# Latent attention's projections as three products of split halves, with the query input written first

## The reference

```python
h = modulate(rmsnorm(x, g_in), shift, scale)          # key side, own shift and scale
kv = h @ w_a                                          # 1024 -> 256 + 64
c_kv, k_rope = jnp.split(kv, [B_KV_LORA], axis=-1)
c_kv = rmsnorm(c_kv, g_latent)
kvb = (c_kv @ w_b).reshape(B_, S, B_HEADS, B_NOPE + B_V)
k_nope, v = jnp.split(kvb, [B_NOPE], axis=-1)
k_rope = apply_rope(k_rope, cos, sin)
...
cq = rmsnorm(h @ w_q_a, g_q_latent)                   # query side, 1024 -> 384
q = (cq @ w_q_b).reshape(B_, S, B_HEADS, B_NOPE + B_ROPE)
q_nope, q_rope = jnp.split(q, [B_NOPE], axis=-1)
```

## Time and profile before

| | before |
|---|---|
| time of three runs | 1122.48, 1123.25, 1126.98 us; median 1123.25 |
| span of the profiled execution | 1122.2 us (no other time is listed for that execution; the median lies 1.05 us above it) |
| TensorE busy | 1051.8 us, 94% |
| VectorE busy | 717.4 us, 64% |
| ScalarE busy | 499.2 us, 44% |
| mean granted TensorE clock | 0.986 |
| HBM read | 202.58 MB, 181 GB/s over the span |

### The profile page before, as it was taken

How to read it: one execution, slowest core, us unless ns; L and a number is a source line. 1 busy time by engine, 2 the same in 40 slices (tenths; PEclk the granted TensorE clock), 3 DMA queues, 4 the chain that set the end, 5 groups by cost and what they waited for, 6 DMA issues and landing times.

```text
span 1122.2 us, 19655 instructions
## 1 busy us (share of the span) xinstructions
PE 1051.8 (94%) x8476; PEld 881.5 (79%) x8476; DVE 717.4 (64%) x1180; ACT 499.2 (44%) x792; POOL 33.2 (3%) x31
## 2 busy tenths in 40 slices
PE   5999999889998989999988999999899889999997
PEld 5884679887787867787766999999557769999995
DVE  6778248738889757655596776776335756644444
ACT  2424132136643576444364535454323745544542
POOL 0000015200000100000000000000000000000000
...
DMA packets 15078, 204.88 MB, mean 183 GB/s; under 512 B 1800, under 2 KB 1800, under 8 KB 2832
## 3 DMA queue, kind: packets, MB, share of 16 engines
...
HBM read 202.58 MB, written 1.05 MB: 181 GB/s over the span
## 4 chain that ended last, share of the span: by engine, by line
PE 78%; DVE 12%; ACT 4%; DMA 3%; issue 2%; SPq 0%; DVEq 0%; ACTq 0%
PE bank L434 15%; PE bank L436 14%; PE bank L435 14%; PE bank L529 8%; PE bank L393 5%; PE bank L745 5%; DMA ring<-in_stream 3%; DVE slot_parts L1846 3%; DVE small L1820 2%; PE bank L542 2%; PE bank L556 2%; PE bank L650 1%; PE bank L729 1%; ACT page_parts L1245 1%; DVE arena L2284 1%
## 5 line engine op out<-in xcount | busy, mean ns | idle before, releaser
L434 PE MATMUL bank<-page_parts 128*128 128x512 f32 (+1 forms) x1104 | 377.4, 342 | 8.6 <-DVE slot_parts L1846 3.8
L1846 DVE TENSOR_TENSOR slot_parts<-ring,page_parts 128x2048 fp32r<-128x2048 f32 x104 | 237.2, 2289 | 115.3 <-ACT page_parts L1245 114.7
L1245 ACT ACTIVATE page_parts<-ring 128x2048 fp32r<-128x2048 f32 x104 | 197.8, 1913 | 133.9 <-PE bank L436 73.2
L434 PEld LDWEIGHTS bank<-page_parts 128*128 128x128 f32 x1104 | 209.9, 190 | 32.8 <-issue 7.5
L436 PE MATMUL bank<-page_parts 128*128 128x512 f32 x576 | 225.1, 391 | 0.0
L435 PE MATMUL bank<-slot_parts,page_parts 128*128 128x512 f32 x576 | 225.0, 391 | 0.0
L1302 ACT ACTIVATE arena<-bank 128x512 f32<-128x512 f32 (+2 forms) x134 | 73.8, 574 | 193.6 <-PE bank L529 70.4
L435 PE MATMUL bank<-page_parts 128*128 128x256 f32 x528 | 149.4, 283 | 0.0
L436 PE MATMUL bank<-page_parts,slot_parts 128*128 128x256 f32 x528 | 149.4, 283 | 0.0
L436 PEld LDWEIGHTS bank<-page_parts 128*128 128x128 f32 x576 | 108.5, 188 | 22.9
L435 PEld LDWEIGHTS bank<-slot_parts,page_parts 128*128 128x128 f32 x576 | 108.6, 189 | 21.5
...
## 6 DMA issues: line engine op xcount, KB each, us to landing
...
pos_i<-in_positions ACTq DMA_DIRECT2D x1, 1.0 KB, 4.0
```

Of the source, the lines that this page charges most:

```text
L434: mm(out, a[0], b[0], start=start, stop=False)
L1245: act(unit_parts(n)[0], unit_values(n)[1], ACT.Copy).then_inc(ac.step("w_hi"), 1)
L1846: tt(unit_parts(n)[1], lo, hi, ALU.subtract).then_inc(dv.step("w_lo"), 1)
```

## The change

Every projection of the latent attention (cq, ckv, qr, qn, kn, v3) now takes split operands and `three`. Its panels are cut into units of unequal size (`split_spans`: 1536, 1536; 1280, 1280, 1536; 1536, 1536; 2048, 2048 columns) and split by ScalarE and VectorE as the MLP's are; q_a's two units are split at the end of the first MLP. The two modulated inputs are split on VectorE (`split_mixed`), the turned latents get a high part from ScalarE (`latent_hi`) and a low part from VectorE (`latent_lo`, straight from PSUM). ScalarE writes the whole query input before the key input. TensorE computes half of qn before the key latent is turned, the other half after.

The diff, cut to its core:

```diff
+            def split_spans(name, *spans):
+
+                order.append([name, None])
+                i = panels[0]
+                panels[0] += 1
+                for n, (a, b, k, on) in enumerate(spans):
+                    units.append({"slot": i, "span": (a, b, k), "page": on, "stage": stage[0], "panel": order[-1], "last": n == len(spans) - 1})
+                return len(units) - len(spans)
 
             stage_first = {}
...
             transposes("hT_d", XN)
             ada_turned()
-            project_tok(("cq",), wt(panel("q_a"), QL), hT2, n=QL, transposed="hT_d")
-            panel_used()
+            stage[0] = "mla"
+            q_a = split_spans("q_a", (0, 1536, 4, 15), (1536, 3072, 4, 16))
+            unit_of["cq"] = q_a
+
+            def latent(name, units_of, src, n, wait):
+
+                bs = [claim((name, tb)) for tb in range(TB)]
+                for i in range(units_of):
+                    W = use_unit()
+                    for tb in range(TB):
+                        unit_of[name, tb] = unit_at[0] - 1
+                        for k in range(4 * i, 4 * i + 4):
+                            if tb == 0 and k % 2 == 0:
+                                pe.wait_ge(sem(wait), k // 2 + 1)
+                            ins = three(bs[tb][:, 0:n], [a[:, k, tb * P:(tb + 1) * P] for a in src], [w[:, k - 4 * i, :] for w in W],
+                                        k == 0, k == KT - 1)
+                        if i == 1 and tb == 0:
+                            ins.then_inc(filled((name, 0)), 1)
+                    ins.then_inc(unit_used((name, 1) if i else None), 1)
+
+            def columns_of(name, half, W, rows, src, last):
+
+                for i in range(2):
+                    b = claim((name, half, i))
+                    unit_of[name, half, i] = unit_at[0] - 1
+                    for hf in range(2):
+                        ct = 2 * i + hf
+                        for k, row in enumerate(rows):
+                            ins = three(b[:, hf * T:(hf + 1) * T], [w[:, row, ct * P:(ct + 1) * P] for w in W], [a[:, k, :] for a in src],
+                                        k == 0, k == len(rows) - 1)
+                    ins.then_inc(unit_used((name, half, i)) if last and i else filled((name, half, i)), 1)
+
+            def rows_of(product, W, rows, src, last):
+
+                for tb in range(TB):
+                    p = (*product, tb)
+                    b = claim(p)
+                    unit_of[p] = unit_at[0] - 1
+                    for k, row in enumerate(rows):
+                        ins = three(b[:, :], [a[:, k, tb * P:(tb + 1) * P] for a in src], [w[:, row, :] for w in W], k == 0, k == len(rows) - 1)
+                    ins.then_inc(unit_used(p) if last and tb else filled(p), 1)
+
+            latent("cq", 2, split_parts(HQ_PAGES), QL, "hT_q_split")
             spread(2)
-            Wa = panel("kv_a")
-            project_tok(("ckv",), wt(Wa, KVL + RD), hkvT2, n=KVL + RD)
+            unit_of["kv_a"] = split_spans("kv_a", (0, 1280, 4, 2), (1280, 2560, 4, 14), (2560, 4096, 3, 15))
+            latent("ckv", 2, split_parts(HKV2_PAGES), KVL + RD, "hT_kv_split")
             pe.wait_ge(sem("cq_n"), 1)
             transposes("cqT", CQ, tiles=3)
-
-            project_tok(("qr",), Wa[:, 2560:4096].rearrange("p (k n) -> p k n", k=3), CQT, k_tiles=3, transposed="cqT")
-            panel_used()
+            W = use_unit()
+            for i in range(2):
+                pe.wait_ge(*evacuated(("cqT", i)))
+            rows_of(("qr",), W, range(3), CQT_PARTS, True)
+            unit_of["q_b"] = split_spans("q_b", (0, 1536, 3, 16), (1536, 3072, 3, 14))
+            columns_of("qn", 0, use_unit(), range(3), CQT_PARTS, True)
             pe.wait_ge(sem("ckv_n"), 1)
             b = claim("ckvT")
             for j in range(2):
...
+            columns_of("qn", 1, use_unit(), range(3), CQT_PARTS, True)
+            unit_of["kv_b"] = split_spans("kv_b", (0, 2048, 4, 15), (2048, 4096, 4, 16))
+            pe.wait_ge(*evacuated("ckvT"))
+            W = use_unit()
             for half in range(2):
-                project_T(("qn", half), Wn[:, half * 1536:(half + 1) * 1536].rearrange("p (k n) -> p k n", k=3), CQT, k_tiles=3)
-            panel_used()
-            Wb = panel("kv_b")
-            pe.wait_ge(*evacuated("ckvT"))
+                columns_of("kn", half, W, (2 * half, 2 * half + 1), CKVT_PARTS, half == 1)
+            W = use_unit()
             for half in range(2):
-                project_T(("kn", half), Wb[:, half * 1024:(half + 1) * 1024].rearrange("p (k n) -> p k n", k=2), CKVT, k_tiles=2)
-            for half in range(2):
-                project_tok(("v3", half), Wb[:, 2048 + half * 1024:2048 + (half + 1) * 1024].rearrange("p (k n) -> p k n", k=2),
-                            CKVT, k_tiles=2)
-            panel_used()
+                rows_of(("v3", half), W, (2 * half, 2 * half + 1), CKVT_PARTS, half == 1)
             ada(3, rest=2)
             pe.wait_ge(sem("qr_rope"), 1)
             transposes("qrT", QR, tiles=4)
...
+                    split(unit_of["cq"] + 1)
...
 
 
             act_.wait_ge(sem("mod"), 4)
-            for i in range(4):
-                act_.wait_ge(*finished(("hT_d", i)))
-                for jj in range(2):
-                    j = 2 * i + jj
-                    for n, (dst, m) in enumerate(((hkvT2, 2), (hT2, 3))):
+            for dst, m in ((hT2, 3), (hkvT2, 2)):
+                for i in range(4):
+                    act_.wait_ge(*finished(("hT_d", i)))
+                    for jj in range(2):
+                        j = 2 * i + jj
                         ins = act(dst[:, j, :], bank(("hT_d", i))[:, jj * T:(jj + 1) * T], ACT.Identity,
                                   scale=MODS[m][0][:, j:j + 1], bias=MODS[m][1][:, j:j + 1])
-                        if (jj, n) == (1, 1):
-                            ins.then_inc(ac.frees(("hT_d", i)), 1)
-                        else:
+                        if jj == 0:
                             ins.then_inc(ac.step(), 1)
-            ada_turned()
+                    ins.then_inc(ac.frees(("hT_d", i)) if m == 2 else ac.step("hT_q"), 1)
+                if m == 3:
+                    split(unit_of["kv_a"])
+                    ada_turned()
+            split(unit_of["kv_a"] + 1)
             for tb in range(TB):
                 copy(CQ[:, tb, :], ("cq", tb), QL)
             for tb in range(TB):
                 copy(CKVR[:, tb, :], ("ckv", tb), KVL + RD)
-            scaled("cqT", CQT, par("q_latent"), tiles=3)
+
+            def latent_hi(product, parts, scale, tiles, first=0):
+
+                act_.wait_ge(*finished(product))
+                for j in range(tiles):
+                    act(parts[0][:, first + j, :], bank(product)[:, j * T:(j + 1) * T], ACT.Copy, scale=scale[:, first + j:first + j + 1]).then_inc(
+                        ac.step("latent_hi"), 1)
+
+            latent_hi(("cqT", 0), CQT_PARTS, par("q_latent"), 2)
+            latent_hi(("cqT", 1), CQT_PARTS, par("q_latent"), 1, 2)
             for tb in range(TB):
                 copy(QR[:, tb, :], ("qr", tb))
-            act_.wait_ge(*finished("ckvT"))
-            for j in range(2):
-                ins = act(CKVT[:, j, :], bank("ckvT")[:, j * T:(j + 1) * T], ACT.Copy, scale=par("kv_latent")[:, j:j + 1])
-                if j == 0:
-                    ins.then_inc(ac.step(), 1)
-            ins.then_inc(ac.frees("ckvT"), 1)
+            for i in range(2):
+                copy(QNT[:, 2 * i:2 * i + 2, :], ("qn", 0, i))
+            latent_hi("ckvT", CKVT_PARTS, par("kv_latent"), 2)
             pair(KRT_OF, "krT", T)
-            for half in range(2):
-                for i in range(2):
-                    copy(QNT[:, 4 * half + 2 * i:4 * half + 2 * i + 2, :], ("qn", half, i))
+            for i in range(2):
+                copy(QNT[:, 4 + 2 * i:6 + 2 * i, :], ("qn", 1, i))
             for half in range(2):
                 for i in range(2):
                     copy(KNT[:, 4 * half + 2 * i:4 * half + 2 * i + 2, :], ("kn", half, i))
...
+            def split_mixed(name, pages, ready):
+
+                value, (hi, lo) = page(pages[0], KT), split_parts(pages)
+                for i in range(4):
+                    js = slice(2 * i, 2 * i + 2)
+                    dve.wait_ge(*ready(i))
+                    V.tensor_copy(hi[:, js, :], value[:, js, :]).then_inc(dv.step(), 1)
+                    dve.wait_ge(*dv.last)
+                    tt(lo[:, js, :], value[:, js, :], hi[:, js, :].bitcast(F32), ALU.subtract).then_inc(dv.step(name + "_split"), 1)
+
+            def latent_lo(product, parts, scale, tiles, done, first=0):
+
+                dve.wait_ge(sem("latent_hi"), done + tiles)
+                for j in range(tiles):
+                    hi, lo = (a[:, first + j, :] for a in parts)
```

(13 more changed lines are left out.)

21 lines of the change are left out of this document (14 added, 7 removed).

## The result

The changed kernel takes 1129.24 us (median of 18 runs, 1125.28 to 1134.58) against 1125.99 us of the kernel before on the same chips (18 runs, 1121.97 to 1127.89). The ratio is 1.0031, 95% interval [1.0018, 1.0043]: within the 0.5% that the prediction counts as no change, though the interval lies above 1. Forecast was 2.55 us on top of the median of the runs shown (0.23%), that is 1125.8. The profiled execution spans 1128.0 us against 1122.2.

What follows compares the result with a forecast made beforehand. TensorE was taken to bound the stage. The walk's +0.2 us and clock drops' +2.4 gave +2.6 on the 1122.2 span, 1124.8, or 1125.8 on the runs' median; own range 1121.5 to 1128.9, 8-in-10 range 1120.0 to 1129.5.

Steps and rivals of the forecast that it cites:

- TensorE's bill: The six latent-attention projections: three reduced-precision matmuls per product take 39.7 us instead of 48.5, relieving TensorE of 8.8 us.
- steps 1 and 2: Stage's beginning: cq ends at 820.8 us instead of 824.3, ckv at 829.7 instead of 834.7.
- step 2: VectorE up to the query statistics: TensorE wins five microseconds, but VectorE's cq is only 1.0 us ahead of before.
- VectorE's bill: Splitting inputs, panels and latents adds 22.9 us on VectorE in the stage, against 31.7 us of room.
- Step 3: Before qr: TensorE stands 3.9 us for VectorE's splits and low parts; qr starts at 835.1 us, before at 836.34.
- Step 4: At the key latent's turn: VectorE stands 3.4 us; its panel sums end at 867.2 us instead of 859.14.
- the walk: Each engine followed in written order through the stage: attention starts at 870.1 us against 869.91, +0.2, good to 2 us.
- Step 5: After v3, ending at 859.7 us: TensorE stands 1.5 and 5.1 us for the sums' columns; scores start at 870.1.
- The clock: After the 3.9 and 5.1 us stalls TensorE's clock drops, costing 0 to 1.7 us each, taken as 1.2: +2.4.
- Rival B: TensorE's clock stays low after the stalls, 6.8 us a drop, costing 3.4 each: +7.0, 1130.3 us; chance 0.14.
- Rival A: If the panel sums were not last, TensorE's 6.6 us in the stage would stay won: 1116.7 us; chance 0.10.
- Rival C: The stalls in the stage take the gain exactly and no clock drop falls on work: 1123.5 us; chance 0.20.

Runs made afterwards that it cites:

- e10_late_only: The changed kernel with cq and ckv put back to full precision, their inputs and panels not split; ratio to the kernel before 1.004.
- e1_warm: The changed kernel with matmuls that nobody reads put into TensorE's three stalls; ratio to the kernel before 0.9998.
- e3_turn_first: The changed kernel with the key latent turned ahead of the first half of qn again; ratio to the kernel before 1.0038.
- e4_sums_gap: The changed kernel with 6 of 16 panel-sum steps moved into VectorE's wait ahead of the key latent's low part; ratio to the kernel before 0.9966.
- e2_no_sums: The changed kernel with 12 of the 16 steps of the two panel sums ahead of the attention left out; ratio to the kernel before 0.997.

## Why the prediction was right

- **Size and sign.** 0.23% slower was forecast, 0.31% [0.18, 0.43] measured. In microseconds it was closer: 1129.24 lies within the 8-in-10 range by 0.3, and above the 1128.9 that was the forecast's own upper bound and its border to "slower". The kernel before measured 1125.99 here, 2.7 above the median of the three runs shown, which is most of the distance to 1125.8; that this shift did not carry the time out of the range is luck, the difference of 0.31% against 0.23% is not.
- **TensorE's bill and steps 1 and 2.** cq was done at 821.1 (823.06 less 1.95), forecast 820.8; ckv's end some 830.1, forecast 829.7. The column prices between the rows' 0.2276 and 0.1215 us held: cq's 48 products start over 8.26 us, 47 times 0.176. Of the 5 us won on cq and ckv VectorE's query statistics show 1.0 (828.09 less 1.95 is 826.1, against 827.16), as step 2 said, and e10_late_only shows qr's start to hang on that split by 0.8.
- **VectorE's bill.** The low parts, for which no row stood, took 0.42 us each (1.26 for three), 0.44 (0.88 for two): within the bounds of 0.3 and 0.69, and above my 0.36.
- **Step 3.** Stall 3.84, forecast 3.9; qr at 835.26 on the scale of before, forecast 835.1.
- **Step 4.** The wait for the key latent was 5.39 instead of 3.4 us, and 3.25 in e1_warm, where TensorE's clock stays up: the walk's wait plus the first drop, which the forecast had put on the path. The forecast put the wait down to qn's move ("which the half of qn has pushed back"); e3_turn_first shows that 1.9 of the 5.39 us hang on it, and that the next wait takes over the rest. That VectorE had work for the gap, which the forecast listed as queued behind it, is what e4_sums_gap used.
- **Step 5.** Stalls 1.16 and 5.00, forecast 1.5 and 5.1. v3 ended at 862.0 where the walk, without drops, had 859.7; in e1_warm it ends 50.26 us after the stage's begin, which is 859.8. Without drops the stage is 62.01 in e1_warm against 61.96 before: +0.05, forecast +0.2.
- **The clock, the mis-sized term.** Each drop was put at 1.2 us, 2.4 together. They cost 2.1 and 1.8, 3.9 together, each above the bound of 1.7, and e1_warm returns 3.9. The 1.2 lay between 0 and the 1.7 of a stretch of 3.4 us all in work, as in the earlier trace rows; here the stretches were 6.8 us each (834.7 to 841.5 and 868.8 to 875.6 by the granted clock), with some 4 us of work in each. Rival B said 6.8 us of work per drop: its length came true, its cost of 3.4 a drop did not, since 2.5 us of each stretch fell into the stall. The Trainium skill, page "TensorE: Matmul & The Clock Gate", section "HAM oscillation — how this bites in real kernels", has each burst of matmuls behind a long pause restart at half rate, and that was nearer than my mean. The traces agree: every unfilled stall of over 3 us in this stage, in every kernel run (3.10, 3.84, 5.00 and 5.01 us), dropped the clock. The prediction's estimate of 3.4 by that page would have given 1126.8.
- **Rival A.** Its condition was right: e2_no_sums, with most of the sums left out, shortens the stage by 4.75 us against before, even with one drop left, and e4_sums_gap, with all of them and six steps moved, by 2.7. In this change it didn't hold. **Rival C's** exact balance is e1_warm's 0.9998.
